# RWKV steps among decode pieces: weights 4, 2, 3 become 19, 15, 9

## The reference: what is computed

```python
proj = x_ext @ w_in                                  # one input projection for both kinds of heads
attn = fox_attend(q, k, v, logf)                     # forgetting attention; the sample rows read 4096 past
                                                     # tokens of a paged cache (8 sequences x 32 pages of 128)
out, S = rwkv7_time_mix(r, k, v, wl, al, gl, S0)     # RWKV-7: decay, key normalisation, then a scan:
#   S = S * w_t + (S @ a_t) b_t + v_t k_t ;  y_t = S @ r_t      group norm and gate of y behind it
h = x + concat(attn, out) @ w_out
h = h + (silu(hn @ w_gate) * (hn @ w_up)) @ w_down
y = rms_norm(h)
```

## Time and profile before

| what | value |
|---|---|
| median of 3 runs | 1493.53 us |
| all runs | 1500.2, 1493.53, 1491.98 us |
| span of the profiled execution | 1488.3 us |
| median of the runs less that span | 5.2 us |
| PE busy | 1385.8 us, 93% of the span |
| PE weight loads busy | 940.9 us, 63% |
| DVE, ACT, POOL busy | 415.7, 377.3, 109.7 us |
| the chain that ended last | 86% PE, 5% DVE, 3% ACT, 3% DMA |

### The profile page before, as it was taken

The page is one execution under the profiler, slowest core; times in us unless marked ns, Lnnn a source line. Parts: engine busy times, 40 slices in busy tenths (PEclk is TensorE's granted clock), DMA queues, the critical chain, the costliest instruction groups (busy, mean ns, idle before and its releaser), DMA issues.

```text
span 1488.3 us, 27779 instructions
## 1 busy us (share of the span) xinstructions
PE 1385.8 (93%) x11531; PEld 940.9 (63%) x11531; DVE 415.7 (28%) x885; ACT 377.3 (25%) x747; POOL 109.7 (7%) x223
## 2 busy tenths in 40 slices
PE   5999999978799999999988879999999999999997
PEld 4755666655577777777745554477777777744442
DVE  5022355444664344433262421300000000000002
ACT  3020233235744454354534431100000000000011
POOL 6283000000000000003001010000000000000000
PEclk8999899998999999999999989999999999999999
DMA  6187011017797786788869795011112311150001
GB/s 209 58 190 200 17 57 36 1 41 243 262 338 255 241 282 223 243 270 246 277 219 365 276 337 177 1 57 57 57 57 70 100 57 57 57 198 0 0 0 63
DMA packets 123174, 219.31 MB, mean 147 GB/s; under 512 B 11451, under 2 KB 35078, under 8 KB 123046
## 3 DMA queue, kind: packets, MB, share of 16 engines
q1 hardware_dynamic: 115154, 193.64, 38.7%
q0 software_dynamic: 7824, 23.85, 5.9%
q10 hardware_dynamic: 68, 0.02, 0.0%
HBM read 203.06 MB, written 14.41 MB: 146 GB/s over the span
## 4 chain that ended last, share of the span: by engine, by line
PE 86%; DVE 5%; ACT 3%; DMA 3%; issue 2%; SPq 1%; POOL 0%; DVEq 0%; POOLq 0%; ACTq 0%
PE PS L1365 23%; PE PS L734 13%; PE PS L1384 10%; PE PS L1176 7%; PE PS L1190 4%; PE PS L1304 4%; PE PS L1235 3%; PE PS L707 2%; PE PS L1390 1%; DMA arena<-in_cache_k 1%; DMA arena<-in_cache_v 1%; PE PS L990 1%; PE PS L994 1%; PE PS L1000 1%; SPq L422 1%
## 5 line engine op out<-in xcount | busy, mean ns | idle before, releaser
L1365 PE MATMUL PS<-arena 128*128 128x288 f32 x1408 | 345.1, 407 | 1.2 <-DVE arena L2250 1.2
L1365 PEld LDWEIGHTS PS<-arena 128*128 128x128 f32 x1408 | 267.6, 190 | 78.5 <-DVE arena L2250 1.4
L734 PE MATMUL PS<-arena 128*128 128x301 f32 (+1 forms) x736 | 195.8, 423 | 0.0
L1618 ACT ACTIVATE arena<-PS 128x512 f32<-128x512 f32 x256 | 141.1, 595 | 164.4 <-PE PS L1176 164.4
L734 PEld LDWEIGHTS PS<-arena 128*128 128x128 f32 (+1 forms) x736 | 135.5, 187 | 53.9 <-issue 12.4
L1176 PE MATMUL PS<-arena 128*128 128x128 f32 x1024 | 149.3, 289 | 19.2 <-DMA arena<-in_cache_k 6.8
L1384 PE MATMUL PS<-arena 128*128 128x512 f32 x352 | 151.5, 592 | 1.5 <-DVE arena L2275 1.5
L1176 PEld LDWEIGHTS PS<-arena 128*128 128x128 f32 x1024 | 117.5, 147 | 48.4 <-issue 26.1
L1384 PEld LDWEIGHTS PS<-arena 128*128 128x128 f32 x352 | 66.5, 189 | 86.3 <-issue 84.3
L2275 DVE TENSOR_TENSOR arena<-PS,arena 128x576 f32<-128x576 f32 x22 | 16.7, 758 | 330.0 <-ACT arena L1691 330.0
L1691 ACT ACTIVATE arena<-PS 128x576 f32<-128x576 f32 x22 | 14.3, 650 | 332.9 <-PE PS L1365 332.9
(11 more groups left out here) (356 smaller groups left out, 1377.6 us busy)
## 6 DMA issues: line engine op xcount, KB each, us to landing
arena<-in_cache_k SPq DMA_DIRECT2D x256, 256.0 KB, 4.2
arena<-in_cache_v SPq DMA_DIRECT2D x256, 256.0 KB, 4.5
arena<-in_w_gate SPq DMA_DIRECT2D x11, 1024.0 KB
arena<-in_w_up SPq DMA_DIRECT2D x11, 1024.0 KB
arena<-in_w_in SPq DMA_DIRECT2D x5, 2048.0 KB, 11.8
forgets_after<-arena POOLq DMA_DIRECT2D x64, 128.0 KB, 8.4
arena<-forgets_after SPq DMA_DIRECT2D x32, 256.0 KB, 5.1
arena<-in_w_down SPq DMA_DIRECT2D x4, 2048.0 KB
```

Source lines behind the costliest of these rows:

```text
L734: ins = mm(PS[0:width, bank, 0:HALF], wring[:, c % 2, k, c0:c0 + width], xnT[:, k, half * HALF:(half + 1) * HALF], start=(k == 0), stop=(k ...
L1365: ins = mm(PS[:, 4 * (f % 2) + 2 * w + half, 0:HO], fring[r % FR][:, c:c + P], hT[:, k, half * HO:(half + 1) * HO], start=(k == 0), stop=( ...
L1618: av(KTs[:, (2 * i + q) % LOT], PS[:, T_USE[("k", L, i, q)] % 2, :].rearrange("p (g n) -> p g n", g=NG), ACT.Copy)\
```

## The change

One line gives the steps other weights. No instruction is added, taken away or altered; the instructions of the steps stand elsewhere among those of decode, on PE, ACT and DVE. The queues of SP and POOL are the same to the last instruction.

```diff
-        COSTS = N_PRE * [4] + (12 + 18 * (NTILE - 1)) * [2] + (23 + 16) * [3]
+        COSTS = N_PRE * [19] + (12 + 18 * (NTILE - 1)) * [15] + (23 + 16) * [9]
```

## The result

The changed kernel took 1511.19 us (median of 4 runs, 1504.7 to 1512.23) against 1492.76 (the three runs of before and one more): a ratio of 1.011, with a 95% interval of 1.007 to 1.015. A second comparison on another occasion gave 1.0089 [1.0063, 1.0115]. So by the two ratios it is 13 to 17 us slower (the medians above differ by 18.4), above the range on record (1480 to 1505) and the forecast (1492.3). The profiled execution took 1512.06 us with a span of 1510.3. Two slow executions, 2357.62 us of the kernel before and 2796.71 us of the second experiment, are in no ratio, though the medians are given over all runs.

What follows compares the result with a forecast made beforehand. PE was taken as the bound, so only its idle time and clock could move: -4.9 us ahead of the recurrence, -2.5 in the tiles, +6.2 in the last part, together -1.2, giving 1492.3 us, range 1480 to 1505.

Steps and rivals of the forecast that it cites:

- The wait at the prompt's state: Last part, ACT L1600 waiting for a store behind w_out: PE stall of 6 us, +2.4, and +1.7 for half clock.
- first stall: Ahead of the recurrence, PE's 4.33 us wait before L1216: shrinks to 1.7 us, -2.6, and -4 for the half clock.
- second stall: Ahead of the recurrence, PE's 5.78 us wait before another L1216: becomes about 3.3 and 1.2 us, -1.3 us.
- DVE's limit: Ahead of tile 0, DVE is busy nearly throughout 37.9 us while PE has 3 to 4 fewer pieces: +3 us.
- Tiles: Tiles: most of PE's 4.8 us of RWKV hand-off waits goes, -3 us; shorter lots with denser loads cost +0.5.
- rival C: Faster: all 11.7 us of PE's idle time in the tiles goes; 1483.6 us, chance 0.28.
- New states, waits: Last part, PE waiting for DVE's masks: 2.0, 0.6, 1.6 and 0.5 us, 4.7 in all, a change of -0.8 us.
- New states, clock: Last part, new states: no wait is long, so the matmuls at half clock go, -3 us.
- Turning the states: Last part: ACT waits 2 us for a store to free its buffer, and PE behind it, +2.7 us.
- second spread: Last part, second spread of norms, L845 to L852: less PE work covers the chain, stall 5.4 us, +1.7.
- B: Slower: every hand-off among the last part's 39 steps is too short, 0.4 us of stall each; 1504 us, chance 0.24.
- A: The forecast: first part and tiles win some 7 us, last part loses 6; 1492 us, 0.48 shared with the DMA-bound case.

Runs made afterwards that it cites:

- the second experiment: Kernel before with weights 2318, 1380, 2069: only the part ahead of the recurrence squeezed, last part about as before; 1502.61 us, ratio 1.0039 [1.0004, 1.0074].
- the run of it alone: Kernel before with weights 2676, 1758, 1097: last part squeezed to 42.8 pieces, ahead of the recurrence as before; 1507.5 us, ratio 1.0061 [1.0034, 1.0087].

## Why the prediction was wrong

Two terms failed by most. The clock of the last part was put at a gain, -3 + 1.7 = -1.3 us, and cost about 9 to 14 us in two profiled executions. The wait at the prompt's state was priced at +2.4 us and grew by 6.3. Part by part:

**Ahead of the recurrence, forecast -4.9 us, profile +2.8.** The first stall did go from L1216 as written out: PE waits 1.15 + 0.30 us for copies and scores there, and nothing at L1216. On the timeline of PE after:

```profile
351.23 1.06 PE L1176 MATMUL PS<-arena 128*128 128x128 f32 x8 [1.15 <-ACT arena L1618]
352.60 0.65 PE L1190 MATMUL PS<-arena 128*32 128x128 f32 x16 [0.30 <-DVE arena L2105]
...
363.91 2.47 PE L852 MATMUL PS<-arena 32*128 32x320 f32 x4 [3.48 <-DVE arena L1873]
```

```profile
357.41 5.64 DVE L1893 TENSOR_TENSOR_SCAN arena<-arena 128x640 f32<-128x640 f32 x4 [2.73 <-ACT arena L1491]
```

The step that failed is "If no stall is long, the stretch at half clock goes too", with its -4. I stopped the chain at the turn L1216. DVE waits for the low-rank copy L1491, runs the scans L1893 for 5.64 us, and only then makes the norm for L852, so PE stands 3.5 us there. The half clock comes at 363.0 in place of 355.8, 6.8 us long in place of 10.2, so less than half of the -4 came. The second stall is 4.4 us at L1190, with 1.3 and 1.7 us more at the next L1190 and L1216, against 3.3 and 1.2 forecast: 7.4 us where 4.5 were written. The wait at DVE's limit, 1.5 us, was inside its bounds, under the +3 taken. The first part alone gave 0.39% [0.04, 0.74], so it is a small loss or next to nothing, and not the gain of a third of a per cent.

**Tiles, forecast -2.5 us, table +5.2.** The waits for hand-offs of RWKV went, as written. What failed is the sentence "The rest of its idle time belongs to decode", read as if it would stay: decode's own waits grew by 7.1 us and those under "issue" at L1013 by 1.8. A piece was priced at PE's busy time alone, and it brought its waits along; counted with them, as estimated above, the tiles come to -1.5 and the forecast there was near. This is what rival C had against it. The Trainium skill (Perfetto Trace Analysis, Identifying the Most-Contended Engine) takes the share of weight loads, beside the share of peak arithmetic, as the measure of headroom in place of matmul busy time. By the weight loads the tiles had 62 us to give, and 40 more pieces made them 49.6 us longer, 43.9 of them busy time of PE. The rows above agree with idle time between matmuls, and not with that measure, as the bound here.

**New states, waits.** Forecast 2.0, 0.6, 1.6 and 0.5 us; measured 2.02, 0, 0.73 and 3.14. The sum, 5.9 against 4.7, was near; that it was is in part luck, since the last wait was six times its forecast.

**New states, clock: this is a step that failed.** "none of them long", and -3 us for the clock. In the profiled execution of the change, 27 us there are at half clock where 6.8 were before; L1105 takes 3.68 us in place of 1.94 twice, where it did once. I had tied half clock to waits of some four microseconds. Here 2.02 us were ahead of it, in a stretch whose matmuls are small (64 rows by 64 columns, 32 columns). The change run again had the same wait of 2.02 us and 17 us at half clock; the kernel with fillers at the later waits had 10 us at the new states and 3.4 behind them. The same order can thus get more or less of it.

**Prompt's state, forecast +4.1 us.** The step that failed is "The loads have more room, so the store may land earlier. I take a PE stall of 6 us". It landed after 19.0 us in place of 18.7. The 4.4 us of lost cover on top of ACT's wait of 5.78 give 10.2 us; the prediction has both numbers and does not add them. ACT's wait is 9.3 us and PE's 9.92, where 6 were taken. Moving the store out of the queue gives 10 to 13 us in the change and about 3 in the kernel before. The difference, 6 to 10 us (the intervals leave some 5 us on each side), is the largest term that a run isolates. It was forecast with the right sign at half the size or so, inside its bound of +9.

**Turning the states and the second spread.** 1.7 us for a forecast of 2.7 more, and 5.04 us at L852 for 5.4. Both sizes were near.

**The last part as a whole** was forecast at +6.2 us: +7.5 of waits and -1.3 of clock. By the profiles it came to +15.5 and, in the second execution, +12.1; the run of it alone gave about 9 with what the tiles lost. Waits other than decode's own grew from 13.2 to 23.7 us, +10.5 for the +7.5; the gap is the prompt's state, which was priced 3.9 us too low, less some terms that came out smaller. Decode's own waits left the part (9.9 to 0.8 us), which is why its idle time grew by 1.7 only. The rest is the clock: PE was busy 13.8 and 8.8 us longer for the same work, with 41 and 24 us more at half. The fillers at the two long waits gave back an estimated 13.7 us in one execution. That the clock costs this much is read from profiles; no median shows it by itself.

**The rivals.** B had the sign, the part and nearly the time (1504 us), but not the mechanism: it needed 0.4 us at each of 38 hand-offs and over 40 us of idle time, and the part idles 24.9 us. Most of the loss there is the wait at the prompt's state and the clock. C and A are out. The tail kept its time, as said. Two sums of the rivals are off. At 0.35 us a hand-off B gives -7.4 + 13.3 = +5.9 us, under the 7.5 that it says is passed; it takes 0.39 us. With the first part at its good bounds (-12.4 in place of -4.9) C gives 1476 us and not 1479, below the range.

**The signs.** None of the three signs of being wrong appeared: the idle time is under 40 us, no wait for cache loads is in the list of the tiles, and the first stall is gone. None of them asked for the clock. Among the things to see, idle time of 9 to 12 us up to tile 0 and 8 in the tiles failed (16.6 and 17.4).

**The sum.** The span was forecast at 1487.1 us and 5.2 us around it were added, from the one execution of before. The execution profiled after has 1.8 us around its span. With as much around the span of before, its profiled execution took about 1490.1 us, some 3 us under its median: its profile was of a quick execution, and that after of one slower than its median.

**What stays open.** Why the clock falls behind a wait of 2 us at the new states in one execution for 20.5 us and in another for 6.8. How the +2.8 and +5.2 us of the profile and the 6 us of the first part by itself fit: the tiles alone were not tried, and the interval of that run is as wide as the question. Why L1013's waits under "issue" grew was not tried either.

## What to carry to other kernels

When work that fills waits is spread anew, price each wait that loses its filler in full, up to the wait that stands behind it, price the filler with its own waits and not by busy time alone, and assume no transfer lands earlier unless a row shows what it is queued behind. Add the clock as a term of its own: in a part whose matmuls are small, each microsecond at half clock cost an estimated 0.3 us or more here, and there were 24 to 41 more of them. Ask what a store is queued behind before giving it cover: moving one issue won back some three quarters of what the whole change had lost, though the kernel before would gain about 3 us of that too. And take more than one profile of a kernel before reading differences of a few microseconds: two executions of one order differed by 17 us in their time at half clock.

## What the runs showed of the hardware

The clock was granted at 0.50 for 20.5 us while PE was busy 19.0 of them, behind a wait of 2.02 us. Up to tile 0, in the same order with the same 13.4 us of idle time, 7.8 us more at half clock made a stretch 3.9 us longer, half a microsecond for each; in the last part it was an estimated 0.31 to 0.37 (13.7 us for 44.3 with fillers, 13.8 for 41 and 8.8 for 24 from before to the change). The Trainium skill (TensorE: Matmul & The Clock Gate, Terms) prices time at half clock at one half; the first number agrees with it, the second is below. A store of 64 KB behind a load of 4096 KB on POOL's queue landed after 18.7 to 19.0 us (before, change and change again), and after 4.4 to 5.5 us ahead of it (three kernels).
